# Prompt attention with keys and values multiplied out per head, beside latent attention for the sample rows

## The reference, cut to what matters

```
def _mla_project(hn, pos, w_in, g_q, g_kv, w_qb, w_uk):
    a = hn @ w_in
    cq = _rmsnorm(a[..., :Q_LORA], g_q)                       # 384
    ckv = _rmsnorm(a[..., Q_LORA:Q_LORA + KV_LORA], g_kv)     # 256, shared by all heads
    krope = _rope(a[..., Q_LORA + KV_LORA:], pos)             # 64
    q = (cq @ w_qb).reshape(..., N_HEADS, QK_NOPE + QK_ROPE)  # 8 heads, 128 + 64
    q_lat = jnp.einsum('bshn,chn->bshc', q[..., :QK_NOPE], w_uk)
    q_rope = _rope(q[..., QK_NOPE:], pos)

def _mla_prompt_attend(q_lat, q_rope, ckv, krope):            # 256 causal rows
    sc = (q_lat . ckv + q_rope . krope) * SOFTMAX_SCALE, masked
    return softmax(sc) @ ckv                                  # 256 per head

def _mla_sample_attend(...):                                  # the same over 1024 cached rows + 4 new

def _mla_output(o_lat, w_uv, w_o):
    o = jnp.einsum('bshc,chv->bshv', o_lat, w_uv)             # 256 -> 128 per head
    return o.reshape(...) @ w_o
```

## Time and profile before

| | us |
|---|---|
| three runs | 1022.34, 1017.47, 1021.18 |
| their median | 1021.18 |
| span of the profiled execution | 1021.9 |
| start to the end of the query tiles | 0 to 57.22 |
| latent queries, first scores | 57.22 to 70.48 |
| heads, sample rows | 70.48 to 126.19 |
| `w_uv` and copies (L1883, L736) | 126.19 to 134.69 |
| output projection, routing, experts, second layer | 134.69 to 1021.9 |

### The profile page before, as it was taken

One profiled execution on the slowest core, in us unless ns is written; L12 is line 12 of the kernel. 1 busy time (PEld: TensorE's weight loads), 2 busy tenths in 40 slices (PEclk: granted clock), 3 DMA queues, 4 the chain that ended last, 5 costly groups with the idle time before them and its releaser, 6 DMA issues.

```text
span 1021.9 us, 14272 instructions
## 1 busy us (share of the span) xinstructions
PE 957.6 (94%) x5563; PEld 609.9 (60%) x5563; DVE 420.3 (41%) x1103; ACT 179.8 (18%) x374; POOL 78.7 (8%) x119
## 2 busy tenths in 40 slices
PE   6989899999979889999999999999799999987797
PEld 5767577555544456744468888999544444432276
DVE  4566323733321235621124878645632222221265
ACT  2123114111112103210012110001311111111123
POOL 2444000000000000000000000000111111110000
PEclk9999999999999989999999999999989999999899
DMA  9958799599999998904444323435789999999921
GB/s 357 371 173 267 271 421 382 224 422 419 420 419 422 419 421 340 424 36 164 165 187 143 116 96 143 168 130 183 281 326 418 419 418 417 418 419 422 352 114 47
DMA packets 56200, 300.30 MB, mean 294 GB/s; under 512 B 10146, under 2 KB 16482, under 8 KB 24130
## 3 DMA queue, kind: packets, MB, share of 16 engines
q1 hardware_dynamic: 45648, 280.13, 68.6%
q0 software_dynamic: 8704, 16.27, 4.7%
q10 hardware_dynamic: 1778, 2.94, 0.8%
HBM read 299.86 MB, written 11.51 MB: 305 GB/s over the span
## 4 chain that ended last, share of the span: by engine, by line
PE 70%; DMA 15%; issue 5%; DVE 3%; POOLq 3%; POOL 1%; ACT 1%; SPq 0%; ACTq 0%; DVEq 0%
DMA ring_sb<-stream 13%; PE ps L2393 9%; PE ps L2250 9%; PE ps L2363 8%; PE ps L2431 7%; PE ps L1931 6%; PE ps L2259 4%; PE ps L1915 3%; PE ps L2019 3%; PE ps L2010 3%; PE ps L2044 2%; PE ps L2052 2%; POOLq L626 2%; PE ps L2236 1%; PE ps L2209 1%
## 5 line engine op out<-in xcount | busy, mean ns | idle before, releaser
L2393 PE MATMUL ps<-hn_sb,ring_sb 128*128 128x288 f32 x384 | 96.3, 407 | 0.0
L2250 PE MATMUL ps<-ring_sb,scr_sb 128*64 128x512 f32 x352 | 81.2, 607 | 7.5 <-DMA ring_sb<-stream 7.4
L2363 PE MATMUL ps<-ring_sb,hn_sb 128*128 128x512 f32 x192 | 83.3, 593 | 0.0
L2393 PEld LDWEIGHTS ps<-hn_sb,ring_sb 128*128 128x128 f32 x384 | 71.6, 190 | 18.7 <-issue 0.4
L1931 PE MATMUL ps<-scr_sb,ring_sb 128*128 128x288 f32 x256 | 64.0, 406 | 0.0
L2363 PEld LDWEIGHTS ps<-ring_sb,hn_sb 128*128 128x128 f32 x192 | 36.3, 190 | 45.0 <-issue 44.8
L2250 PEld LDWEIGHTS ps<-ring_sb,scr_sb 128*64 128x64 f32 x352 | 24.9, 140 | 61.5 <-issue 46.7
L1931 PEld LDWEIGHTS ps<-scr_sb,ring_sb 128*128 128x128 f32 x256 | 48.6, 190 | 13.4
L1426 DVE SCALAR_TENSOR_TENSOR scr_sb<-ps,scr_sb 128x256 f32<-128x256 f32 x16 | 7.7, 484 | 118.4 <-ACT scr_sb L853 118.4
L2431 PE MATMUL ps<-scr_sb,ring_sb 128*128 128x144 f32 x384 | 51.0, 286 | 0.0
L2010 PE MATMUL ps<-scr_sb 128*128 128x128 f32 (+1 forms) x384 | 49.0, 280 | 1.9 <-issue 1.9
(11 more groups left out here) (381 smaller groups left out, 1397.7 us busy)
## 6 DMA issues: line engine op xcount, KB each, us to landing
ring_sb<-stream SPq DMA_DIRECT2D x194, 1024.0 KB, 19.6
scr_sb<-stream SPq DMA_DIRECT2D x46, 1024.0 KB, 21.8
ring_sb<-row_pages POOLq DMA_DIRECT2D x64, 128.0 KB, 5.1
hn_sb<-stream SPq DMA_DIRECT2D x8, 1024.0 KB, 22.5
scr_sb<-key_pages SPq DMA_DIRECT2D x24, 192.0 KB, 8.9
ring_sb<-key_pages SPq DMA_DIRECT2D x24, 192.0 KB, 6.0
scr_sb<-y_rows SPq DMA_DIRECT2D x4, 512.0 KB, 5.8
scr_sb<-b_v SPq DMA_DIRECT2D x1, 1920.0 KB, 7.8
```

What stands on the lines that cost most here:

```text
L2250: last = mm(ps[64 * a:64 * a + 64, 2 + b, :], xT[:, k, 64 * a:64 * a + 64], slot(k // 2)[:, (k % 2) * D + a * 512:(k % 2) * D + a * 512 + ...
L2363: last = mm(v_bank(unit), hn_t[:, k, P * t:P * t + P], ring(s, k % 4 * 512, 512), start=(k == 0), stop=(k == KD - 1))
L2393: last = mm(bank((i + 1) % 4, T), ring(s, (i % 2) * D + k * P, P), hn_t[:, k, :], start=(k == 0), stop=(k == KD - 1))
```

## The change

Prompt rows get keys and values per head. `v_tile(t)` makes the values of 128 prompt rows for all heads (4 matmuls of 512 columns), `k_pair(p)` the keys of two heads (4 matmuls of 256 columns), from `ckvT` and from `w_uk` in a second layout (`un`, the new input `uk_n`) and an early copy of `w_uv` (`uv_e`). `scores` then has two matmuls per block instead of three, `apply_p` two instead of four, and its result goes straight into `oT`. Latent queries are made for the 32 sample rows alone (`q_latent`, 16 matmuls of 32 columns), as is the step through `w_uv` at the end (16 matmuls of 32 columns and one copy). The six transposes of L1748 shrink to two, for the sample rows, behind `q_latent`. SP issues three transfers more: `uv_e` (1 MB) and `un[1]` (0.5 MB) behind slot 6, and `un[0]` (0.5 MB), into memory that the input projection reads, behind key chunk 2. Semaphores of POOL's later work are merged under one name.

```
         for s in range(S_IN + 2, S_UK + 1):
             load_slot(s)
+        sp.dma_start(uv_e, stream[stream_row(S_UV)]).then_inc(sem("uv_in"), 16)
+        sp.dma_start(un[1], io["uk_n"][1]).then_inc(sem("uv_in"), 16)
         sp.wait_ge(sem("par_in"), 32)
-        for chunk in (0, 1, 2, 3, 4, 6):
+        for chunk in (0, 1, 2):
+            load_keys(sp, chunk)
+        sp.wait_ge(sem("a_ps"), 6)
+        sp.dma_start(un[0], io["uk_n"][0]).then_inc(sem("half_in"), 16)
+        for chunk in (3, 4, 6):
             load_keys(sp, chunk)
...
-        take_ql(0, 6)
+        take_kp(0)
+        take_kp(2)
         exp_prompt(0)
-        take_ql(6, H)
         exp_prompt(1)
+        act.wait_ge(sem("vp_ps"), 5)
+        nc.scalar.activation(ckt, ps[0:NS_, 7, 0:KV], ACT.Copy).then_inc(sem("vp_sb"), 1)
...
-        take_ql(0, 6)
+        take_kp(1)
+        take_kp(3)
         max_prompt(0)
-        take_ql(6, H)
-        norm_prompt(0)
         max_prompt(1)
-        dve.wait_ge(sem("ql_a"), H)
-        dve.wait_ge(sem("ql_d"), H)
+        dve.wait_ge(sem("kq_ps"), H // 2 + 1)
         for c in range(2):
             nc.vector.tensor_copy(qs[:, c].rearrange("p b (h s) -> p b h s", h=H),
-                                  ql[:, :, c, NP_:T].rearrange("p h (b s) -> p b h s", b=DEC_B)).then_inc(sem("qs"), 1)
+                                  ps[:, 2, c * KV:(c + 1) * KV].rearrange("p (h b s) -> p b h s", h=H, b=DEC_B)).then_inc(sem("qs"), 1)
...
+        norm_prompt(0)
         for h in range(H):
...
+        def v_tile(t):
+            pe.wait_ge(sem("uv_in"), 32)
+            for half in range(2):
+                if t:
+                    pe.wait_ge(sem("vp_sb"), half + 1)
+                for c in range(2):
+                    last = mm(bank(6 + half), ckvT[:, c, P * t:P * t + P], uv_e[:, c * D + 512 * half:c * D + 512 * half + 512],
+                              start=(c == 0), stop=(c == 1))
+                last.then_inc(sem("vp_ps"), 1)
+        def k_pair(p):
+            pe.wait_ge(sem("uv_in" if p // 2 else "half_in"), 32)
+            if p < 2:
+                pe.wait_ge(sem("vp_sb"), 3 + p)
+            else:
+                pe.wait_ge(sem("q_sb"), Q_AT["r", p])
+            for e in range(2):
+                for c in range(2):
+                    at = ((2 * p + e) % 4 * 2 + c) * P
+                    last = mm(ps[:, KP_BANK[p], e * NP_:(e + 1) * NP_], un[p // 2][:, at:at + P], ckvT[:, c, 0:NP_],
+                              start=(c == 0), stop=(c == 1))
+                    if e == 0 and c == 0:
+                        free_with(last)
+            last.then_inc(sem("kq_ps"), 1)
+        v_tile(0)
+        for tile in Q_SEQ[4:8]:
+            q_tile(tile)
+        v_tile(1)
+        for tile in Q_SEQ[8:]:
             q_tile(tile)
         owe(3)
...
-            pe.wait_ge(sem("ql_a"), h + 1)
-            pe.wait_ge(sem("ql_d"), h + 1)
+            pe.wait_ge(sem("kp_d" if h // 2 % 2 else "kp_a"), h // 4 + 1)
             for c0, q0, kn in ((0, 0, P), (P, P, NP_)):
-                free_with(mm(ps[:, u, c0:c0 + kn], ql[:, h, 0, q0:q0 + P], ckvT[:, 0, 0:kn], start=True, stop=False))
-                mm(ps[:, u, c0:c0 + kn], ql[:, h, 1, q0:q0 + P], ckvT[:, 1, 0:kn], start=False, stop=False)
+                free_with(mm(ps[:, u, c0:c0 + kn], qn[:, h, q0:q0 + P], kp[:, h, 0:kn], start=True, stop=False))
                 last = mm(ps[:, u, c0:c0 + kn], qr[:, h // 2, q0:q0 + P], kz[:, h % 2, 0:kn], start=False, stop=True)
...
-            for c in range(2):
-                mm(ps[:, 3, c * NP_:(c + 1) * NP_], ckt[:, 0, c * P:(c + 1) * P], pt_p[:, 0:NP_], start=True, stop=False)
-                last = mm(ps[:, 3, c * NP_ + P:(c + 1) * NP_], ckt[:, 1, c * P:(c + 1) * P], pt_p[:, NP_:384], start=False, stop=True)
+            at = h % 2 * NP_
+            mm(ps[:, 3, at:at + NP_], vp[:, 0, h * P:(h + 1) * P], pt_p[:, 0:NP_], start=True, stop=False)
+            last = mm(ps[:, 3, at + P:at + NP_], vp[:, 1, h * P:(h + 1) * P], pt_p[:, NP_:384], start=False, stop=True)
...
-        ql_tiles(0, 4)
-        scores(0)
-        ql_tiles(4, 6)
-        scores(1)
-        ql_tiles(6, H)
+        for p in range(H // 2):
+            k_pair(p)
+        scores(0)
+        scores(1)
+        wait_slots(pe, S_UK, S_UK + 1)
+        q_latent()
...
         for h in range(H):
-            if h >= 4:
-                pe.wait_ge(sem("o_sb"), h - 3)
             for c in range(2):
-                last = mm(bank(h % 4, T), ring(S_UV, c * D + h * P, P), ql[:, h, c, :], start=(c == 0), stop=(c == 1))
-            last.then_inc(sem("o_ps"), 1)
+                last = mm(ps[:, 0, h * NS_:(h + 1) * NS_], ring(S_UV, c * D + h * P, P), ols[:, h, c, :], start=(c == 0), stop=(c == 1))
+        last.then_inc(sem("o_ps"), 1)
```

More of the change, by code:

```diff
@@ L182, in program @@
     krn = A.take(NS_, RO)
-    ckt = A.take(3 * KV).rearrange("p (t c) -> p t c", t=3)
-    ql = A.take(H * 2 * T).rearrange("p (h c t) -> p h c t", h=H, c=2)
+    ckt = A.take(KV, NS_)
+    work = A.take(H * 2 * T)
+    pt_s = A.take(9 * P).rearrange("p (g r) -> p g r", g=9)
+    early = A.at
     s_p = A.take(2 * 384).rearrange("p (b n) -> p b n", b=2)
@@ L733, in _ @@
                 copy_pts(h // 4)
-        for h in range(H):
-            act.wait_ge(sem("o_ps"), h + 1)
-            nc.scalar.activation(oT[:, h, :], bank(h % 4, T), ACT.Copy).then_inc(sem("o_sb"), 1)
+        act.wait_ge(sem("o_ps"), 1)
+        nc.scalar.activation(oT[:, :, NP_:T], ps[:, 0, 0:H * NS_].rearrange("p (h t) -> p h t", h=H), ACT.Copy
+                             ).then_inc(sem("o_sb"), 1)
         def route_rows(L, rows, total, logit):
@@ L1745, in _ @@
         pe.wait_ge(sem("std"), 3)
-        for t, (t0, tn) in enumerate(TOK):
-            for c in range(2):
-                last = nc.tensor.transpose(ps[0:tn, 6 + t // 2, (t % 2) * KV + c * P:(t % 2) * KV + c * P + P],
-                                           ckvT[:, c, t0:t0 + tn], ident)
-        last.then_inc(sem("ckt_ps"), 1)
-        for tile in Q_SEQ[4:]:
+        def v_tile(t):
+            pe.wait_ge(sem("uv_in"), 32)
+            for half in range(2):
+                if t:
[4 more added lines that the diff above has]
+                last.then_inc(sem("vp_ps"), 1)
@@ L1752, in _, with q_latent @@
+        def q_latent():
+            for h in range(H):
+                for c in range(2):
+                    at = c * KV + h * NS_
+                    last = mm(ps[:, 2, at:at + NS_], ring(S_UK, h * KV + c * P, P), qn[:, h, NP_:T], start=True, stop=True)
+            last.then_inc(sem("kq_ps"), 1)
+        v_tile(0)
[3 more added lines that the diff above has]
+        for tile in Q_SEQ[8:]:
             q_tile(tile)
         owe(3)
-        def ql_tiles(h0, h1):
-            for h in range(h0, h1):
-                for c in range(2):
-                    if h >= 2:
-                        pe.wait_ge(sem("ql_a" if c == 0 else "ql_d"), h - 1)
-                    last = mm(bank(QL_BANK[(2 * h + c) % 4], T), ring(S_UK, h * KV + c * P, P), qn[:, h, :], start=True, stop=True)
-                    if c == 0:
-                        free_with(last)
-                last.then_inc(sem("ql_ps"), 1)
```

79 lines of the change are left out of this document (46 added, 33 removed).

## The result

| | before | after |
|---|---|---|
| median of the comparison (20 runs each) | 1020.68 us | 1024.17 us |
| lowest to highest | 1016.69 to 1025.23 | 1018.45 to 1029.47 |
| ratio, 95% interval | | 1.0033 [1.0018, 1.0049] |
| span of the profiled execution | 1021.9 us | 1024.1 us |
| output projection starts | 134.69 us | 138.82 us |

The change made the kernel slower: 3.5 us between the medians, 3.4 by the ratio. The forecast was 1019.5 us, slightly faster; the range, 1012 to 1026, holds the time. The change is within the 0.5% that the prediction called no change, but twenty runs a side tell its sign, and the sign was forecast wrong.

What follows compares the result with a forecast made beforehand. POOL's page issues bound the attention layer up to chunk 7, PE after it. +4.2 (POOL) - 1.3 (applies) - 4.7 (w_uv step) = -1.8 us from 1021.18 gave 1019.4, stated as 1019.5; range 1012 to 1026.

Steps and rivals of the forecast that it cites:

- What bounds the kernel: Attention: POOL's page issues set when PE gets key chunk 7 (107.72 us); the layer's end time passes on in full.
- The prediction's own test of its premise: Premise is wrong if the output projection moves by one amount and the end of the first experts by another.
- The change to POOL: POOL's 41st page waits for the query projection's slots, freed later by PE; chunk 7 lands 4.2 us later, at 111.9.
- Transfers: SP's 2.1 MB of extra loads arrive before PE asks: un[1] at 35.6 us, un[0] about 57.5; nothing added at the experts.
- Rival (b): At k_pair(0): un[0] lands after 62.4 us and delays POOL further, at the latest 66.0; 1023.0 us, chance 0.12.
- the term of -4.7 us: Step through w_uv: 16 matmuls cut from 288 to 32 columns at 0.20 us each, 3.3 us instead of 8.01.
- Behind chunk 7: PE's work after key chunk 7: two applies save 1.3 us, the w_uv step saves 4.7 us.
- rival (c): TensorE's clock falls in the heads; at half clock behind chunk 7, 1.7 to 3.5 us more, 1021 to 1023; chance 0.13.
- The term of -1.3 for the two applies: Behind chunk 7, the applies of heads 6 and 7 take 0.65 us less each.
- Rival (a): POOL isn't late, or by less: sum -6.0, 1015.2 us, or 1012.6 with cheaper 32-column matmuls; chance 0.20.
- (d): Per-head work brings PE to chunk 7 after 111.9; each us over 2.3 counts; chance 0.55 together with the forecast.

Runs made afterwards that it cites:

- the waits filled: Changed kernel plus five 512-column matmuls that compute nothing, put into PE's waits before the first head and key chunks 5 and 7: 1.0021 of before, 1022.93 us.
- the version with the order mended: Changed kernel with both value tiles moved behind the last query tile, so the first value matmul frees the slots: 0.9984 of before, median 1019.4 us.
- both costs mended: Changed kernel with value tiles behind all query tiles and 128 columns moved per matmul in the w_uv step: 0.9941 of before, 1014.63 us.

## Why the forecast was wrong

**What bounds the kernel: right.** Chunk 7's landing set PE's restart, and the attention layer handed its time on: what stood at the second pass stood at the experts' first matmul too (before 187.1, after 193.1 us). The prediction's own test of its premise was the end of the first experts: the last of their final matmuls (L2052, now L2096) starts at 399.7, 396.6 and 397.1 us in the three profiles of before and at 404.0, 404.9 and 404.9 in those of after, 6.8 us later on the mean, against 6.7 at the second pass.

**The change to POOL: right, in place and size.** +4.2 us forecast, +4.17 measured at chunk 7; putting the delay alone into the kernel before cost 5.1 us at the second pass and 0.38% of the time. But POOL was not alone: with the delay removed (values behind queries) PE takes up chunk 7 near 109.8 and not at 107.72, so 2.1 of the 4.2 us are PE's own lateness, hidden behind POOL's delay. `k_pair`, `q_latent` and `turn_p(0)` came at 62.57, 72.09 and 78.37 us, forecast 62.4, 71.9 and 77.9.

**Transfers: right.** `un[0]` landed at 58.0 us (forecast 57.5), ahead of the matmul that asks at 62.57; `un[1]` at 36.1 (forecast 35.6). Rival (b) is out. SP's weight loads started at 118.23, 6.9 us later than in the earlier trace rows and not 4.2, for the slower matmuls behind chunk 7, and SP still waited 17.8 us for a slot at the experts.

**The `w_uv` step: this is the step that failed, the term of -4.7 us.** "I take 0.20, the row of the same weights: 16 are 3.3 with the end, and 8.01 - 3.3 = 4.7 saved". The price itself was fair: at full clock the 16 products of `q_latent`, of the same shape, took 3.65 us. But the term took the clock for granted. The sixteen 32-column products took 0.41 us each, nearly all of them at 1.2 GHz, and the slow clock reached 3.8 us into the output projection (3.3 to 4.9 in the six profiles). The saving was 1.5 and not 4.7 us, and 1.9 of it went again in the projection, whose term I had not written at all. Net +0.4 for a term of -4.7. With 128 columns the step costs 3.81 us, 0.16 more than 32-column products at full clock, and the clock holds: then 8.50 with its copy becomes 4.34, a saving of 4.2.

**Behind chunk 7: rival (c) came true, at +3.1 us** (19.97 against 16.90 with the waits filled), within its own 1.7 to 3.5. The term of -1.3 for the two applies was right in kind and measured -1.6 (16.90 against 18.47). I gave (c) 0.13, because each wait was shorter than the 2.84 us idle in the earlier trace rows. That compares one wait with a sum of several. PE's timeline of before there:

```profile
373.04 1.07 PE L2019 MATMUL ps<-ring_sb,scr_sb 128*32 128x512 f32 x8 [1.33 <-DMA ring_sb<-stream]
375.52 1.07 PE L2019 MATMUL ps<-ring_sb,scr_sb 128*32 128x512 f32 x8 [1.42 <-DMA ring_sb<-stream]
378.01 1.93 PE L2019 MATMUL ps<-ring_sb,scr_sb 128*32 128x512 f32 x8 [1.42 <-DMA ring_sb<-stream]
```

No single wait was over 1.42 us, and the clock fell in the third; the 2.6 and 2.3 us that the prediction saw ahead of chunks 5 and 7 were longer, and spoke for (c). Measured, PE stood idle for 1.98 us ahead of chunk 7 and had been busy for 27.18 of the 31.80 us from 80 us on; the clock fell in all three profiles of after, and not behind the filled waits. (c) alone would have given about +1.0; with the thin step it is the +4.1 at the projection's start. The Trainium skill, "TensorE: Matmul & The Clock Gate", section "HAM oscillation — how this bites in real kernels", puts the falling clock of a kernel whose product has few rows down to its waits on DMA. The fills bear out that kind of cause for the stretch behind chunk 7, though the waits that the page shows are longer, some 3 to 5 us, than the 1.98 to 2.25 us here. The stretch in the `w_uv` step is not of this kind: nothing waited for DMA there, the waits ahead of it are the same with 128 columns, and the fills left it; a forecast by that rule would have had the same -4.7.

**Rival (a) and (d).** POOL was late, so (a) is out as a forecast; the version with the order mended shows what it would have been, and it isn't the -6.0 I gave it: the second pass comes 0.9 us later than before, and the time falls by 0.16% (1.6 us between 1021.0 and 1019.4). The clock in the `w_uv` step is one part of this. The other is a contradiction in the prediction: it had PE ready for chunk 7 at 109.6, and still let (a) start there at 107.72, which leaves out 1.9 us. With both costs mended the second pass is 3.5 us earlier than before. (d) did not come: PE was ready for chunk 7 at 109.9 (forecast 109.6).

**What stays open.** At the second pass the three profiles of after stand 5.9 to 7.3 us behind those of before (152.45, 153.50 and 153.27 against 146.43, 146.21 and 146.57), their spans 5.3 us on the mean, the medians 3.5. On the mean nothing is given back by the end of the first experts. What is given back behind them and what is the scatter of single executions (the three spans of before go from 1016.8 to 1021.9), I did not settle. Nor did I measure matmuls of 64 columns, or fewer than sixteen thin ones in a row. The version with 128 columns also spreads the results over two banks of `ps` instead of one; no run parts this from the columns. And since the clock falls early in the `w_uv` step, it isn't shown whether 32-column products would bring it down there without the waits ahead; at `q_latent` they did so in four profiles of ten.

## What to carry to other kernels

When work is put between a buffer's last load and the instruction that frees it, look at who waits for the buffer: with a queue that issues one page in 1.14 us and is the bound, each us of delay is a us at the next stage (5.2 late, 5.1 there), and the work belongs behind the freeing instruction. Ask as well what bounds once the delay is gone: here PE itself, 2.1 us later. A matmul whose price its weights set gains next to nothing from fewer columns, and a run of them can cost the clock, for itself and for the dense work behind: keep them at 128 columns. (To spread them was not tried.) And a term at one clock is half a term: write the sum at both levels wherever a change thins out TensorE's work.
